# Norm scaling moved behind the products, reordered splits, a three-pass input product and spread late queries in a one-core transformer kernel

## The chip, the cores and the metric

The kernel is one program on one core of a Trainium2 chip. The metric is the device time of one execution in microseconds (us), median of three runs. Everything is fp32 with a sequence of 256 tokens and a model width of 1024.

## The reference, cut to what matters

Two layers of a first kind are followed by one layer of a second kind.

```python
def rms_norm(x, g):
    y = x * lax.rsqrt(jnp.mean(x * x, axis=-1, keepdims=True) + 1e-6)
    return y * g

for layer in range(2):
    x = x + 0.5 * swiglu(rms_norm(x, norm_ffn1[layer]), gate, up, down)   # swiglu: (silu(x@gate) * (x@up)) @ down
    xn = rms_norm(x, norm_mix[layer])
    x = x + mix(xn @ w_in) @ w_out[layer]       # layer 0: stick-breaking and block attention, layer 1: forgetting and dilated
    x = x + 0.5 * swiglu(rms_norm(x, norm_ffn2[layer]), gate, up, down)
# last layer
u = rmsnorm(x, g_mix) @ w_in                    # 2336 columns for two branches, 2048 for their gates
x = x + (gated rwkv7 recurrence and latent attention of u) @ w_out
h = rmsnorm(x, g_ffn)
q = h @ w_q                                     # 8 heads, top 16 of 128 x 128 keys each
x = x + sum_e gate_e * gelu(expert_u[e] . h) * expert_v[e]    # rows gathered for each token
x = x + sigmoid(rmsnorm(x) @ w_ple_gate) * (p @ w_ple_proj)   # side projection, then a final norm
```

## The kernel before

**Layout.** `xT` holds x transposed, eight chunks of 128 channels by 256 tokens. Weights stream from HBM through a ring of six slots of 1 MB (`ring`, filled by SP at L628, each fill waiting until the slot's last reader is done: `freed`). Every matmul is issued at L704.

**Split products.** The four feed-forward stages (`ffn(0)` to `ffn(3)`) and the two input products of the mixers (`layer`) split both operands into a high and a low fp32r part and take three passes (`mm3`: high by high, low by high, high by low). ACT makes the high part of a weight slot (L1384 in an FFN, L1391 in a mixer), DVE the low part (L1756, L1761). The gate and up weights have two pairs of buffers, the down weights one pair; ACT waits for `pair_used` before it overwrites a pair.

**Norms 0 to 5** stand ahead of the four FFNs and the two mixers. In order: DVE adds the last product to `xT` in four pieces (L1809 or L1816); ACT squares each piece (L1405); PE sums the squares over channels with a matmul by ones (`ssq`); ACT takes the inverse root by Ln and Exp (L1409, L1411, `rstd`); DVE multiplies x by the gain and by `rstd` (L1775); ACT takes the high part (L1415, `xh`), DVE the low part (L1779, `xl`); PE starts the next product.

**An FFN** has 22 chunks of 128 hidden channels in 11 groups of two. PE takes gate and up of chunk c, then down of chunk c - 1. ACT takes the silu of the gate bank (L1432), DVE the product with the up bank (L1792), ACT its high part (L1434), DVE its low part (L1795). After each even chunk both engines split one down slot, after each odd one a gate and an up slot. The order on each engine is the order written.

**A mixer's input product** has 12 slots. ACT evicts the query and key banks (L1520), DVE the value banks (L1913).

**The last layer's input product** (`second_in`) takes plain fp32 matmuls on `xn`, straight from the ring: nine slots of 256 columns and one of 32. ACT evicts (L1570) and DVE forms shifted sums after 5, 10 and 15 of the 19 pieces.

**The experts** run over 16 units of (128 tokens, one head). POOL gathers 16 u rows of a unit and, between them, 16 v rows of the unit before (L2356), 512 KB each, into 7 and 8 buffers. DVE takes the dot products with the u rows (L2234), ACT the softmax weights and gelu (table loads at L1693 and L1697), DVE the weights of the unit before after its fourth u row (L2221). ACT makes diagonal matrices (L1705) and PE adds diagonal times v row (`weighted_rows`). Queries and scores of six heads come first. Those of heads 6 and 7 and the side projection come in one block behind `weighted_rows(0)`, on PE and on ACT.

## Time and profile before

| | |
|---|---|
| median of three runs | 2450.94 us (2449.79 to 2454.59) |
| profiled execution | 2459.51 us, its span 2457.8 us |
| granted TensorE clock, mean | 0.925 |
| PE busy | 2106.7 us, 86% of the span |
| DVE, ACT, POOL busy | 1200.8, 787.8, 678.1 us |
| chain that ended last | PE 68%, POOL 10%, issue 6%, DVE 6%, DMA 4%, ACT 3% |

The chain says which engine the end waited for at each moment. A share of busy time says less, since the stages have different limits. The sum of a change is best made stage by stage, from the windows and the timeline at the places where PE or POOL stands still.

### The profile page before, as it was taken

What the parts mean: (1) busy time and instruction counts of PE and PEld (TensorE: products, weight loads), DVE (VectorE), ACT (ScalarE), POOL (GpSimd) and SP (SyncE); (2) the same over time, 40 slices, a digit from 0 to 9 for tenths busy, and PEclk for the clock granted to TensorE, in tenths of its full rate; (3) what the DMA queues carried; (4) which work ended last, traced back from release to release, by engine and by line L of the source; (5) the groups of instructions that cost most, each with busy time, mean ns of one, the idle gap of its engine ahead of it and who ended that gap; (6) DMA issues with size and microseconds to landing.
All of it is one profiled execution on the core that took longest, in us unless ns stands there. A gap on an engine that the chain in (4) does not pass through costs nothing.

```text
span 2457.8 us, 34543 instructions
## 1 busy us (share of the span) xinstructions
PE 2106.7 (86%) x13812; PEld 1680.0 (68%) x13812; DVE 1200.8 (49%) x2250; ACT 787.8 (32%) x1321; POOL 678.1 (28%) x702
## 2 busy tenths in 40 slices
PE   7999989999999999999995999986867667667677
PEld 7999878998999878999773887872422222223235
DVE  5455426445455434453336443285465566566432
ACT  4444535335344533443133223121222121212122
POOL 0000010000001000000006321047477777777770
PEclk9999999999999959999996997998888989878999
DMA  8554316554554305553420100579599999999990
GB/s 293 190 191 129 119 52 206 188 171 155 188 183 142 121 1 169 184 191 116 124 76 17 36 20 19 173 258 396 201 374 342 360 373 366 346 373 364 358 371 31
DMA packets 253787, 489.56 MB, mean 199 GB/s; under 512 B 13872, under 2 KB 173136, under 8 KB 253536
## 3 DMA queue, kind: packets, MB, share of 16 engines
q0 software_dynamic: 73888, 268.53, 29.2%
q1 hardware_dynamic: 176016, 214.32, 26.9%
q10 hardware_dynamic: 3760, 5.02, 0.6%
q8 instruction: 84, 1.38, 0.2%
q14 instruction: 39, 0.32, 0.0%
HBM read 486.74 MB, written 1.05 MB: 198 GB/s over the span
## 4 chain that ended last, share of the span: by engine, by line
PE 68%; POOL 10%; issue 6%; DVE 6%; DMA 4%; ACT 3%; another core or an unknown queue 1%; DVEq 0%; ACTq 0%; POOLq 0%
PE bank L704 67%; POOL arena_sb L2356 8%; POOL con_sb L2356 2%; DMA con_sb<-peer_v,arena_sb 1%; DMA arena_sb<-peer_u,arena_sb 1%; DVE parts_sb L1756 1%; DMA arena_sb<-peer_v,arena_sb 1%; DVE sq_sb L1775 1%; PE bank L851 1%; DVE xl_sb L1779 1%; ACT parts_sb L1384 1%; DVE arena_sb L2023 0%; DVE arena_sb L2103 0%; DMA xT_sb<-xT 0%
## 5 line engine op out<-in xcount | busy, mean ns | idle before, releaser
L704 PE MATMUL bank<-arena_sb 64*64 64x64 f32 (+8 forms) x3704 | 554.9, 338 | 195.2 <-ACT arena_sb L1705 119.3
L704 PE MATMUL bank<-xh_sb,parts_sb 128*128 128x256 f32 x3328 | 608.4, 285 | 19.0 <-DVE xl_sb L1779 11.9
L704 PEld LDWEIGHTS bank<-arena_sb 64*64 64x64 f32 (+4 forms) x3704 | 330.8, 172 | 415.6 <-issue 259.9
L704 PEld LDWEIGHTS bank<-xh_sb,parts_sb 128*128 128x128 f32 x3328 | 515.2, 190 | 29.6 <-issue 19.1
L704 PE MATMUL bank<-xl_sb,parts_sb 128*128 128x256 f32 x1664 | 469.5, 282 | 0.0
L2234 DVE CUSTOM_DVE_ANT_0 sq_sb<-arena_sb 128x1024 f32<-128x1024 f32 x256 | 309.6, 1224 | 265.2 <-DMA arena_sb<-peer_u,arena_sb 249.1
L1756 DVE TENSOR_TENSOR parts_sb<-ring_sb,parts_sb 128x2048 fp32r<-128x2048 f32 x132 | 298.6, 2290 | 192.2 <-ACT parts_sb L1384 192.2
L2356 POOL DMA_INDIRECT arena_sb<-peer_u,arena_sb x256 | 272.1, 1063 | 194.7 <-DVE arena_sb L2204 110.6
L704 PEld LDWEIGHTS bank<-xl_sb,parts_sb 128*128 128x128 f32 x1664 | 316.5, 190 | 0.0
L1384 ACT ACTIVATE parts_sb<-ring_sb 128x2048 fp32r<-128x2048 f32 x132 | 247.9, 1910 | 96.5 <-PE bank L704 95.1
L704 PE MATMUL bank<-xn_sb,ring_sb 128*128 128x256 f32 (+1 forms) x1200 | 271.1, 386 | 8.4 <-DVE xn_sb L1775 4.9
L704 PEld LDWEIGHTS bank<-xn_sb,ring_sb 128*128 128x128 f32 (+1 forms) x1200 | 229.3, 193 | 47.0 <-issue 14.4
L704 PE MATMUL bank<-h_high_sb,parts_sb 128*128 128x256 f32 x1408 | 256.2, 283 | 1.6 <-DVE parts_sb L1756 1.6
L704 PE MATMUL bank<-con_sb,arena_sb 128*128 128x512 f32 (+1 forms) x512 | 185.3, 511 | 52.2 <-DMA con_sb<-peer_v,arena_sb 50.2
L704 PEld LDWEIGHTS bank<-h_high_sb,parts_sb 128*128 128x128 f32 x1408 | 218.2, 190 | 2.3 <-DVE parts_sb L1756 2.2
L1705 ACT ACTIVATE arena_sb<-con_sb,arena_sb 128x128 f32<-128x128 f32 x256 | 90.2, 395 | 387.9 <-PE bank L704 158.6
L2356 POOL DMA_INDIRECT arena_sb<-peer_v,arena_sb x160 | 181.9, 1137 | 84.3 <-PE bank L704 43.0
L704 PE MATMUL bank<-h_low_sb,parts_sb 128*128 128x256 f32 x704 | 198.6, 282 | 0.0
L704 PEld LDWEIGHTS bank<-con_sb,arena_sb 128*128 128x128 f32 (+1 forms) x512 | 73.6, 176 | 159.6 <-issue 159.6
L1432 ACT ACTIVATE sgate_sb<-bank 128x256 f32<-128x256 f32 x88 | 33.8, 384 | 324.4 <-PE bank L704 324.4
L704 PEld LDWEIGHTS bank<-h_low_sb,parts_sb 128*128 128x128 f32 x704 | 134.1, 191 | 0.0
L2356 POOL DMA_INDIRECT con_sb<-peer_v,arena_sb x96 | 117.7, 1226 | 37.7 <-issue 24.1
(246 smaller groups left out, 1718.6 us busy)
## 6 DMA issues: line engine op xcount, KB each, us to landing
ring_sb<-ffn_w_gate SPq DMA_DIRECT2D x44, 1024.0 KB, 5.5
ring_sb<-ffn_w_up SPq DMA_DIRECT2D x44, 1024.0 KB, 6.6
ring_sb<-ffn_w_down SPq DMA_DIRECT2D x44, 1024.0 KB, 4.9
ring_sb<-w_in SPq DMA_DIRECT2D x17, 1024.0 KB, 5.3
ring_sb<-w_in_ab SPq DMA_DIRECT2D x12, 1024.0 KB, 5.2
ring_sb<-w_out SPq DMA_DIRECT2D x12, 1024.0 KB, 5.1
ring_sb<-w_in_cd SPq DMA_DIRECT2D x12, 1024.0 KB, 5.4
ring_sb<-peer_w_q SPq DMA_DIRECT2D x8, 1024.0 KB, 5.4
```

The source lines that it names most:

```text
L704: return pe.matmul(dst, lhsT, rhs, start=start, stop=stop_, skip_group_check=loose)
L851: ins = pe.transpose(b[:, dst : dst + P], pr[:, src : src + P], ident)
L1384: act.activation(whi(kind, g), ring[:, k % RING, :], ACT.Copy).then_inc(hi_ready, 1)
L1432: act.activation(sgate[:, c % 2, :], bank[4 + c % 2][:, 0:T], ACT.Silu).then_inc(silu_ready, 1)
L1705: act.activation(DG[n % ND], ident, ACT.Copy, scale=WT[:, tb, 16 * h + e : 16 * h + e + 1]).then_inc(S("diag_ready"), 1)
L1756: dve.tensor_tensor(wlo(kind, g), ring[:, k % RING, :], whi(kind, g), ALU.subtract).then_inc(split_ready, 1)
L1775: dve.scalar_tensor_tensor(out=raw[:, k, :], in0=xT[:, k, :], scalar=V(name, c0 + k), in1=rstd[:, :], op0=ALU.mult, op1=ALU.mult).then_inc ...
L1779: dve.tensor_tensor(xl[:, k - 2, :], sq[:, k - 2, :], xh[:, k - 2, :], ALU.subtract).then_inc(xn_ready, 1)
L2234: dve.tensor_tensor_reduce(JUNK[n % 2], UROW[n % NU], HTOK[:, tb, :], 1.0, 0.0, ALU.mult, ALU.add, DOTS[:, tb, 16 * h + e : 16 * h + e + 1 ...
L2356: pool.indirect_dma_start(out=row[n % len(row)], out_offset=None, in_=A[table][0], in_offset=bass.IndirectOffsetOnAxis(ap=EIDX[:, tb, 16 * ...
```

## The change

**Norms 0 to 5.** The product no longer waits for the inverse root. ACT writes `xh` as the high part of x times gain, straight from `xT` and ahead of the squares; DVE makes `xl` in one operation (x times gain minus `xh`), between the residual pieces. PE takes the first gate product (or the first value half) and only then the sum of squares. The root is applied where the product leaves its bank. In an FFN, DVE scales gate and up together (128x512) and the silu and the product read the result in SBUF. In a mixer, DVE evicts queries and keys times `rstd`, and values times a column of it that PE makes by two small matmuls (`rcol`). The squares and `MIX` get places of their own in the arena.

**Splits.** The first slot of a mixer and the first gate and up slots of `ffn(2)` are split after chunk 20 of the FFN before; those of `ffn(1)` and `ffn(3)` by DVE ahead of the residual; the second up slot after chunk 0.

**Last layer's input product.** Nine slots are split (two pairs of buffers) and take three fp32r passes; `xn` is split by ACT and DVE after the norm.

**Experts.** Query pieces 12 to 15 stand behind `weighted_rows(0)` to `(3)`, one each, and the two halves of the side projection behind `(4)` and `(5)`.

```diff
-        MIX = xn
+        MIX = view(24064, KC, T)
+        SQX = {n: view(0 if n in (1, 4) else 22016, KC, T) for n in range(6)}
+        RCOL = small[:, 160:162]
+        GU = [sgate, hT]
...
+        LATE = {0: ("query", 12), 1: ("query", 13), 2: ("query", 14), 3: ("query", 15), 4: ("ple", 0), 5: ("ple", 4)}
...
+                            if c == 0 and j + kk == 0:
+                                release(first)
...
+                        if c == 0 and j == 0:
+                            norm(n)
...
+                        if s == 0 and half == 0:
+                            norm(1 + 3 * l)
+                        if s == 0 and half == 1:
+                            b = fill_begin(pe, ("rcol", l))
+                            pe.wait_ge(S("rstd_ready"), 2 + 3 * l)
+                            for tb in range(2):
+                                ins = mm(b[:, tb : tb + 1], rstd[0:1, tb * P : (tb + 1) * P], C("ones", 1)[0:1, :], True, True)
+                            fill_end(ins, ("rcol", l))
...
+                                first, ins = mm3(b[:, 0:T], w[0][:, kk, cols], w[1][:, kk, cols], x2h[:, kk, :], xl[:, kk, :],
+                                                 kk == 0, kk == KC - 1)
...
+                    if u in LATE:
+                        kind, m = LATE[u]
+                        if kind == "query":
+                            query(m)
+                        else:
+                            projection(m)
...
+            def high_in2(s):
+                k, base = at["in2",] + s, SPLIT0["in2",]
+                act.wait_ge(slot_loaded[k % RING], 16 * (k // RING + 1))
+                if s > 1:
+                    act.wait_ge(pair_used, base + s - 1)
+                act.activation(in2_hi(s), ring[:, k % RING, :], ACT.Copy).then_inc(hi_ready, 1)
...
-                    high_qkv(n // 3, 0)
-                if f is not None and f > 0:
-                    if n in (2, 5):
-                        take(act, ("y", n // 3, 0))
+                if n in (2, 5):
+                    take(act, ("y", n // 3, 0))
                     high(f, "gate", 0)
                     high(f, "up", 0)
                 act.preload_act_table_set("natural_log_exp_and_others")
+                if n <= 5:
+                    name, c0 = norm_g[n]
+                    for m in range(4):
+                        residual_done(act, n, [m])
+                        for k in (2 * m, 2 * m + 1):
+                            act.activation(xh[:, k, :], xT[:, k, :], ACT.Copy, scale=V(name, c0 + k)).then_inc(xh_ready, 1)
+                    if n == 0:
+                        high(0, "gate", 0)
                 for m in range(4):
                     residual_done(act, n, [m])
-                    act.activation(sq[:, 2 * m : 2 * m + 2, :], xT[:, 2 * m : 2 * m + 2, :], ACT.Square).then_inc(sq_ready, 1)
-                if n == 0:
-                    high(0, "gate", 0)
+                    dst = SQX[n] if n <= 5 else sq
+                    act.activation(dst[:, 2 * m : 2 * m + 2, :], xT[:, 2 * m : 2 * m + 2, :], ACT.Square).then_inc(sq_ready, 1)
+                if n > 5:
+                    root(n)
...
-                high(f, "up", 1)
+                root(n)
...
+                    act.wait_ge(scaled, base + c + 1 + 4 * i)
+                    act.activation(gate, gate, ACT.Silu).then_inc(silu_ready, 1)
                     act.wait_ge(hraw_ready, base + c + 1 + 4 * i)
-                    act.activation(HH[:, c % 2, :], hT[:, c % 2, :], ACT.Copy).then_inc(hh_ready, 1)
+                    act.activation(HH[:, c % 2, :], h, ACT.Copy).then_inc(hh_ready, 1)
+                    if c == 0:
+                        high(f, "up", 1)
                     for kind, g in splits_after(c):
                         high(f, kind, g, i)
+                    if c == CHUNKS - 2 and f in (0, 2):
+                        high_qkv(f // 2, 0)
+                    if c == CHUNKS - 2 and f == 1:
+                        high(2, "gate", 0)
+                        high(2, "up", 0)
...
-                    if s >= 4:
-                        for _, _, m in chunks_of(l, s):
-                            b = take(act, ("qk", l, m))
-                            give(act.activation(QK[:, m, :], b[:, 0:T], ACT.Copy), ("qk", l, m))
...
+                for k in range(KC):
+                    act.wait_ge(xn_ready, KC * 6 + k + 1)
+                    act.activation(x2h[:, k, :], xn[:, k, :], ACT.Copy).then_inc(S("x2h_ready"), 1)
+                high_in2(1)
...
+            def low_x(n, m):
+
+                name, c0 = norm_g[n]
+                for k in (2 * m, 2 * m + 1):
+                    dve.wait_ge(xh_ready, KC * n + k + 1)
+                    dve.scalar_tensor_tensor(out=xl[:, k, :], in0=xT[:, k, :], scalar=V(name, c0 + k), in1=xh[:, k, :],
+                                             op0=ALU.mult, op1=ALU.subtract).then_inc(xn_ready, 1)
...
-                    dve.wait_ge(silu_ready, base + c + 1 + 4 * i)
+                    gate, h = GU[c % 2][:, 0, :], GU[c % 2][:, 1, :]
+                    dve.wait_ge(gu_ready, base + c + 1 + 4 * i)
                     if base + c >= 2:
                         dve.wait_ge(h_ready, base + c - 1 + 4 * i)
-                    dve.tensor_tensor(hT[:, c % 2, :], sgate[:, c % 2, :], bank[4 + c % 2][:, T : 2 * T],
-                                      ALU.mult).then_inc(hraw_ready, 1)
+                    dve.tensor_tensor(GU[c % 2][:, :, :], bank[4 + c % 2][:, :].rearrange("p (a b) -> p a b", a=2),
+                                      rstd[:, :].unsqueeze(1).broadcast_to([P, 2, T]), ALU.mult).then_inc(scaled, 1)
+                    dve.wait_ge(silu_ready, base + c + 1 + 4 * i)
+                    dve.tensor_tensor(h, gate, h, ALU.mult).then_inc(hraw_ready, 1)
                     dve.wait_ge(hh_ready, base + c + 1 + 4 * i)
-                    dve.tensor_tensor(HL[:, c % 2, :], hT[:, c % 2, :], HH[:, c % 2, :], ALU.subtract).then_inc(h_ready, 1)
+                    dve.tensor_tensor(HL[:, c % 2, :], h, HH[:, c % 2, :], ALU.subtract).then_inc(h_ready, 1)
+                    if c == 0:
+                        low(f, "up", 1)
...
+                    if m and n < 5:
+                        low_x(n + 1, m - 1)
+                if n < 5:
+                    low_x(n + 1, 3)
...
+                            give(dve.tensor_scalar(VT[:, j % 2, 4 * (j // 2) : 4 * (j // 2) + 4, 0:HD],
+                                                   b[:, 0:T].rearrange("p (a c) -> p a c", a=4), RCOL[:, j % 2 : j % 2 + 1],
+                                                   None, ALU.mult), ("v", l, j))
...
+                    else:
+                        for _, _, m in chunks_of(l, s):
+                            b = take(dve, ("qk", l, m))
+                            give(dve.tensor_tensor(QK[:, m, :], b[:, 0:T], rstd[:, :], ALU.mult), ("qk", l, m))
+                    if s == 0:
+                        low_qkv(l, 2)
...
+                low(2 * l + 1, "gate", 0)
+                low(2 * l + 1, "up", 0)
+                residual(("y", l), 3 * l + 2)
...
+                for k in range(KC):
+                    dve.wait_ge(S("x2h_ready"), k + 1)
+                    dve.tensor_tensor(xl[:, k, :], xn[:, k, :], x2h[:, k, :], ALU.subtract).then_inc(S("x2_ready"), 1)
+                low_in2(1)
...
+                    for s in ((2, 3), (4, 5, 6), (7, 8))[g]:
+                        low_in2(s)
```

## Rows read from the trace of the kernel before

**Rows 1.** The page's slices: DMA share in 40 equal parts of the span.

```profile
DMA  8554316554554305553420100579599999999990
```

**Rows 2.** Windows: us, PE, PEld, DVE, ACT, POOL busy, PE clock, DMA share, GB/s.

```profile
212.50:228.15 15.65, 11.68 (x67) 10.29 (x65) 11.32 (x21) 10.55 (x16) 0.00 (x0) 0.89 0.20 67
368.50:390.60 22.10, 17.94 (x113) 15.81 (x111) 18.55 (x25) 12.72 (x18) 0.00 (x0) 0.92 0.71 224
567.40:591.00 23.60, 17.51 (x114) 16.11 (x112) 18.66 (x26) 14.93 (x22) 0.00 (x0) 0.93 0.49 160
591.00:767.80 176.80, 176.75 (x1488) 176.76 (x1489) 83.00 (x73) 72.47 (x73) 0.00 (x0) 1.00 0.54 175
1720.00:1750.00 30.00, 24.23 (x88) 18.18 (x89) 6.56 (x25) 11.76 (x30) 1.45 (x2) 0.79 0.16 56
1748.00:2400.00 652.00, 453.57 (x951) 183.76 (x951) 370.73 (x909) 127.72 (x304) 498.40 (x447) 0.88 0.97 360
```

**Rows 3.** Windows of PE alone around norm 1 and norm 6: PE busy, clock, DMA.

```profile
216.10:219.50 3.40, 0.62 (x4) 1.00 0.81 265
219.50:223.50 4.00, 3.89 (x17) 0.59 0.11 37
1154.40:1156.00 1.60, 0.03 (x1) 1.00 0.00 0
```

**Rows 4.** Timeline of norm 1: start, us, engine, line, operation, idle before.

```profile
210.51 2.85 DVE L1809 SCALAR_TENSOR_TENSOR xT_sb<-bank,xT_sb 128x512 f32<-128x512 f32 x4 [1.83 <-PE bank L704]
...
212.47 3.61 PE L704 MATMUL bank<-sq_sb,con_sb 128*128 128x256 f32 x16
...
216.12 0.47 ACT L1409 ACTIVATE std_sb<-bank,con_sb 128x256 f32<-128x256 f32 x1 [2.10 <-PE bank L704]
...
218.84 0.36 PE L704 MATMUL bank<-parts_sb,xh_sb 128*128 128x256 f32 x1 [2.75 <-DVE xl_sb L1779]
...
228.15 0.39 PE L704 MATMUL bank<-parts_sb,xh_sb 128*128 128x256 f32 x1 [1.06 <-DVE parts_sb L1761]
```

**Rows 5.** Timeline of an odd and an even chunk inside ffn(1).

```profile
462.42 4.49 DVE L1756 TENSOR_TENSOR parts_sb<-ring_sb,parts_sb 128x2048 fp32r<-128x2048 f32 x2 [1.39 <-ACT parts_sb L1384]
...
467.83 0.39 ACT L1432 ACTIVATE sgate_sb<-bank 128x256 f32<-128x256 f32 x1 [3.64 <-PE bank L704]
...
470.70 1.92 ACT L1384 ACTIVATE parts_sb<-ring_sb 128x2048 fp32r<-128x2048 f32 x1 [1.57 <-PE bank L704]
```

**Rows 6.** Timeline of the first splits of ffn(1) up to its first down product.

```profile
386.31 1.91 ACT L1384 ACTIVATE parts_sb<-ring_sb 128x2048 fp32r<-128x2048 f32 x1
...
388.26 2.29 DVE L1756 TENSOR_TENSOR parts_sb<-ring_sb,parts_sb 128x2048 fp32r<-128x2048 f32 x1 [1.39 <-ACT parts_sb L1384]
...
390.60 0.51 PE L704 MATMUL bank<-h_high_sb,parts_sb 128*128 128x256 f32 x2 [0.55 <-DVE parts_sb L1756]
```

**Rows 7.** Groups by line and form: count, busy us, mean ns, idle before.

```profile
L1405 ACT ACTIVATE sq_sb<-xT_sb 128x512 f32<-128x512 f32 x40 | 23.9, 626 | 68.9 <-DVE xT_sb L1816 66.5 <-DVE xT_sb L1809 1.7
...
L1697 ACT ACT_TABLE_LOAD x16 | 20.5, 1283 | 0.3
...
L1415 ACT ACTIVATE xh_sb<-sq_sb 128x256 fp32r<-128x256 f32 x48 | 19.8, 417 | 13.6 <-DVE sq_sb L1775 13.6
...
L1903 DVE TENSOR_TENSOR arena_sb<-bank,con_sb 128x512 f32<-128x512 f32 x8 | 5.5, 686 | 4.0 <-PE bank L704 3.9
```

**Rows 8.** Timeline of norm 6 and the last layer's input product.

```profile
1155.42 3.25 DVE L1775 SCALAR_TENSOR_TENSOR xn_sb<-xT_sb,vec_sb,rstd_sb 128x256 f32<-128x256 f32 x8 [3.71 <-ACT rstd_sb L1411]
...
1156.05 65.97 PE L704 MATMUL bank<-xn_sb,ring_sb 128*128 128x256 f32 x304 [1.62 <-DVE xn_sb L1775]
```

**Rows 9.** Timeline of the experts: the late block, and a later unit's start.

```profile
1719.91 0.66 ACT L1679 ACTIVATE arena_sb<-bank 128x256 f32<-128x256 f32 x2 [34.29 <-remote]
...
1748.25 0.94 POOL L2356 DMA_INDIRECT arena_sb<-peer_v,arena_sb  x1 [30.87 <-PE bank L704]
...
1881.64 10.97 PE L704 MATMUL bank<-arena_sb 128*128 128x512 f32 x20 [11.30 <-ACT arena_sb L1705]
```

**Rows 10.** Waits from 1760 to 2400 us: total, times, longest.

```profile
ACT arena_sb L1705 <- issue: 86.9, 43, 12.4
```

More of the change, by code:

```diff
@@ L1411, in norm, with ffn @@
                 act.activation(rstd[:, :], std[:, :], ACT.Exp, scale=-0.5).then_inc(S("rstd_ready"), 1)
[L1412 to L1417 removed]
+            def ffn(f, n):
                 base = CHUNKS * f
@@ L1534, in layer @@
                 if l == 1:
-                    b = take(act, ("forget", 1))
+                    emptied(act, ("forget", 1))
                     act.wait_ge(S("bf_loaded"), 16)
-                    chain.link(act, act.activation(FG[0:8, 0, :], b[0:8, 0:T], ACT.Abs, bias=small[0:8, 40:41]))
+                    chain.link(act, act.activation(FG[0:8, 0, :], FG[0:8, 2, :], ACT.Abs, bias=small[0:8, 40:41]))
                     chain.link(act, act.activation(FG[0:8, 0, :], FG[0:8, 0, :], ACT.Exp, scale=-1.0))
@@ L1705, in experts @@
                         act.activation(DG[n % ND], ident, ACT.Copy, scale=WT[:, tb, 16 * h + e : 16 * h + e + 1]).then_inc(S("diag_ready"), 1)
[L1706 to L1711 removed]
+                    if u in LATE:
+                        kind, first = LATE[u]
+                        if kind == "query":
+                            query_out(first)
+                        else:
+                            for m in range(first, first + 4):
+                                b = take(act, ("pp", m))
+                                give(act.activation(PLE[:, m, :], b[:, 0:T], ACT.Copy), ("pp", m))
                     if h == 7:
@@ new lines, in low_x, with ffn @@
+            def low_x(n, m):
[4 more added lines that the diff above has]
+                                             op0=ALU.mult, op1=ALU.subtract).then_inc(xn_ready, 1)
+            def ffn(f, n):
+                base = CHUNKS * f
+                if f == 0:
+                    for m in range(4):
+                        low_x(0, m)
+                    low(0, "gate", 0)
+                    low(0, "up", 0)
@@ L1799, in ffn @@
+                    if c == CHUNKS - 2 and f == 1:
+                        low(2, "gate", 0)
+                        low(2, "up", 0)
                 for c in range(3):
```

222 lines of the change are left out of this document (110 added, 112 removed).

## The prediction

> **What bounds the kernel now.** The windows come first. Inside an FFN PE is busy for 176.75 of 176.80 us and pulls 1488 matmuls, 0.119 us each; DVE works 83 us there and ACT 72 [rows 2]. So PE sets the FFNs, and only where PE stands still or works less can time be won. It stands still at the norms: 15.65 us pass around norm 1, 22.10 around norm 2 and 23.60 around norm 3, with 11.68, 17.94 and 17.51 of PE in them, part of it at the low clock [rows 2]; norm 4 repeats norm 1 and norm 5 norm 2 to 0.1 us, so these are five places. The slices show the other bound: the DMA engines are 9 tenths busy from slice 27 on, but for one slice with 5 [rows 1]. The experts are bound by gathering (share 0.97 over 652 us), and between 1720 and 1750 the share is 0.16 [rows 2]. That hole is 0.84 x 30 = 25.2 us of lost transfer. POOL waits 30.87 us there for a v buffer, and ACT 34.29 us before it evicts the first late query [rows 9].
>
> **Norm 1, the pattern.** Before, the last down product ends at 212.47, the sum of squares takes 3.6, the root starts at 216.12, the first product at 218.84, and slot 1 of the mixer starts at 228.15 after a wait for its split [rows 4]. After, DVE has from 210.51 on four residual pieces (2.85 together [rows 4]) and eight low parts. Each is one operation of the kind of L1775, eight of which take 3.25 [rows 8]. ACT's eight high parts at 0.42 [rows 7] run between them. The last low part is there at 210.51 + 2.85 + 3.25 = 216.6, the first half product ends at 217.0, fed at DVE's pace. The squares (4 x 0.63 [rows 7]) are ready by then but for the last, and PE sums them until 220.6. The second half takes 24 x 0.119 = 2.85, the column of the root 0.3: slot 1 could start at 223.7.
>
> The split moved into chunk 20 costs something. In an even chunk the down slot's high part starts 2.9 us after the silu and takes 1.92 [rows 5]. DVE then has its low part and one more, 4.49 together [rows 5], so it is free 9.3 us after the silu of chunk 20, and chunk 21's bank is full after 72 x 0.119 = 8.6. Chunk 21's chain is now scaling (priced by L1903, 0.69 [rows 7]), silu 0.39, and three operations of 0.42: some 2.5 us. PE wants it 2.85 after the bank is full; it comes 0.5 late. Slot 1 starts at 224.2 instead of 228.15: 3.9 won, twice (norms 1 and 4).
>
> **Norms 2 and 5.** From the end of the output product E (368.5) only one residual piece and four low parts are left on DVE, about 2.6 us. First gate product ends E + 3.0, sum of squares E + 6.6, up product E + 9.5. Then the splits bind. Chunk 0's chain up to its high part takes 2.0; ACT makes two high parts (1.91 each [rows 6]) and DVE two low parts behind the first (4.49): E + 9.5 + 2.0 + 1.9 + 4.5 = E + 17.9, that is 386.4. PE could start the down product at E + 15.2, so a wait of 2.7 takes the place of the 0.55 before. Before it started at 390.60 [rows 6]: 4.2 won, twice.
>
> **Norm 3.** Two slots are split in chunk 20, so DVE has 6.7 us of low parts and the last down product comes 2.7 late. From E = 570.1 the pattern of norm 1 gives the up product's end at E + 11.0 and the splits as above E + 19.4 = 589.5, against 591.0 [rows 2]: 1.5 won. Norm 0 waits for the first weights; I take nothing, at most 2. Sum of the five: 17.7 us.
>
> **The steady FFN is not slowed.** Scaling adds 0.73 per chunk to DVE. After an odd chunk the two low parts end at 466.91 and the next silu starts at 467.83 [rows 5]: 0.9 free. In an even chunk ACT waits 1.57 us for the down buffer [rows 5], so 1.1 more of chain is free. What hides the 88 scalings (61 us of DVE) is this idle time; without that cover each group would pay up to 1.5 us, 66 in all.
>
> **The clock.** In norm 1 PE stood still for 2.75 us [rows 4], and the granted clock then fell to a mean of 0.59 for 4 us, mostly the lower level, 1.2 GHz [rows 3]. A gap of 1.6 us ahead of norm 6's product left it at 1.00 [rows 3]. Before, the low clock cost little, since DVE's pace ruled then. After, the gaps in the first product are each below 1 us, but it is followed by PE-bound work. A fall costs half of 3.5 us. I take 1.7 us at norms 1 and 4 and nothing elsewhere: 3 (bounds 0 and five falls, 8.5). The Trainium skill's "TensorE: Matmul & The Clock Gate" (section on the HAM clock gate) says that the low rate is the default and sustained activity releases it; by that rule alone a half-fed first product would lose the clock each time, and the norms would give 9 us instead of 15.
>
> **Norms together: 17.7 - 3 = 14.7 won.**
>
> **Last layer's input product.** 152 plain matmuls took 65.97, 0.434 each [rows 8]. 144 of them become three passes of 0.119: 144 x (0.434 - 0.356) = 11.2 won. The start is later: DVE has a low part of a slot first (2.29), which ends 1.1 after the old start of `xn`, then all eight pieces of `xn` (3.25) before the first low part (0.42); in place of 0.6 after 1155.42 PE starts 4.9 after it: 4.3 lost. PE then stood still for 5.9 us, so the low clock costs 1.7. In the stage a slot takes PE 5.7 us and ACT plus DVE 4.7. The shifted sums (about 5 us on DVE, ahead of the low parts of slots 4 and 7) make those two 0.6 late each. 11.2 - 4.3 - 1.7 - 1.2 = 4.0 won (1 to 6.5). The waits on `split_ready` instead of PE free ring slots earlier; SP's loads stay ahead.
>
> **Evictions.** DVE takes the query and key banks. Per slot it then has 0.8 + 2.3 + 0.75 + 2.1 = 6 us against 7.4 of PE with the two small products. The forget gate adds one link, 0.4 lost.
>
> **Experts.** Late pieces now have the gap that PE has at a unit's start, 11.30 us of waiting for ACT's diagonals [rows 9]. Behind a query (8 x 0.434 = 3.5 us, 7 at the low clock) ACT needs an eviction, two table loads (1.28 each [rows 7]) and two short ones, 3.6. So 7.7 is free and a piece fits, barely with scores behind it. The first one meets ACT's late start. If ACT again goes on only at 1719.91 [rows 9], its diagonals come at 1724 and POOL goes on at 1726 instead of 1748.25. POOL's wait shrinks from 30.9 to 8.5, and the transfers in flight ran until about 1725 (0.16 x 30 = 4.8 after 1720), so 2.5 us of hole stays. The other five pieces I give 1.7 together. 25.2 - 4.2 = 21 won. Bounds: 25 if all is hidden, 8 if each of the five costs another 3.
>
> **The sum.** 14.7 + 4.0 - 0.4 + 21 = 39.3. The profiled execution took 2459.51, span 2457.8, which is 0.35% above the median; the sum is a difference of stages and I put it on the median: 2450.9 - 39.3 = 2411.6.
>
> **Rivals.**
> - *The late pieces cost again.* ACT waits of up to 12.4 us for nothing that the trace shows stand between its diagonals (86.9 in 43 waits [rows 10]). If such a wait meets most pieces, the hole returns in parts and only 4 of 21 us are won: 2429. For it: the 34.29 [rows 9]. Against: POOL has 8 v rows of room.
> - *Everything fits.* No fall of the clock, no wait of ACT at the first piece, sums in second_in hidden: 17.7 + 7 + 25 = 50: 2401; with norm 0, 2398.
> - *Slower.* The place is ACT behind `weighted_rows(0)` to `(5)`: a piece sits ahead of the next unit's gelu, which now waits for PE. Its price is piece 7 + wait 12.4 + 3.6 - 11.3 = 11.7 per unit, 70 in six, against 25.2 + 18.3 won: 2451 + 27 = 2478. It decides from 7.3 us per piece. Against: the gap of 11.3.
> - *The chain of a chunk binds.* If five operations with their hand-overs take 1 us more than priced, over 44 groups up to 0.6 each: 26 lost, 2438. Against: rows 5.
> - *The clock falls at each norm* (the skill's rule, above): 6 more lost, 2418; it lies within the forecast's range.
> - *No effect*: the transitions only move their wait and pieces cost as much as the block: 2451.
>
> **Chances.** Forecast (2403 to 2422) 0.50, the clock's case 0.08 in addition, late pieces 0.15, all fits 0.12, the chain 0.05, slower 0.06, no effect 0.04. To leave out no more than 2 in 10 the range goes from 2394 to 2432. What a measurement of this kernel can tell from no change is about 0.2%, 5 us: faster 0.90, same 0.04, slower 0.06.
>
> **What the profile after would show.** Windows from the down product's end to slot 1 of the mixer of 11.7 us instead of 15.7, and 18 instead of 22.1 at norms 2 and 5. At the first down product of `ffn(1)` a PE wait of about 2.7 us for DVE; in chunk 21 of `ffn(1)` one of 2.7. No wait of PE inside the FFNs. The input product in 54 to 57 us, starting about 5 later. No DMA hole above 5 us around the former 1720 to 1750, and POOL waits on PE below 10 us. The prediction is wrong if POOL's waits come back at the first six units, if PE waits inside every FFN group, or if the clock stays low through `ffn`'s first chunk.

## The result and the profile after

The changed kernel takes 2426.85 us, median of four runs (2423.39 to 2431.57), against 2452.77 for the kernel before in the same session. The ratio is 0.9893, with a 95% interval of 0.9866 to 0.9921: 26 us faster, where 39 were forecast. The time lies inside the range (2394 to 2432) but above the likeliest case's own (2403 to 2422).

The profiled execution took 2426.50, span 2424.8, 33.0 less than the span before. The page's slices of the changed kernel, in the order PE clock and DMA share:

```profile
PEclk9999999999999969999987998998998898789899
DMA  8554416554554404554320100579998999999990
```

The slice of 5 tenths inside the experts [rows 1] is gone. What happened elsewhere is read from milestones. This table is put together from the starts and ends of timeline rows (first and last down product of each FFN on PE, last residual piece on DVE, the first 64-row product of an attention, the last layer's first sum of squares, the first sum of squares behind the recurrence); "stage" is the difference of neighbours, in us.

```
stage                                  before    after     won
start to first down product of ffn(0)   35.68    39.09    -3.41
rest of ffn(0)                         176.95   179.68    -2.73
norm 1 and the input product            85.69    81.25     4.44
attention 0, output product             70.35    70.05     0.30
norm 2 to the first down product        21.93    17.79     4.14
rest of ffn(1)                         176.95   182.77    -5.82
norm 3 to the first down product        23.49    18.99     4.50
rest of ffn(2)                         176.96   179.18    -2.22
norm 4 and the input product            95.86    91.54     4.32
attention 1, output product             88.24    83.29     4.95
norm 5 to the first down product        21.93    17.79     4.14
rest of ffn(3)                         176.94   178.43    -1.49
norm 6 and the last input product       73.76    69.98     3.78
latent attention                        96.45    96.10     0.35
recurrence and branches                271.90   267.61     4.29
experts                                814.22   799.30    14.92
side projection, final norm             50.49    51.96    -1.47
```

Attention 1, the recurrence and the ending, 8 of the 33 us, are not put down to the change. Nothing in the recurrence or the ending was edited, and from the end of `ffn(3)` to the last residual ahead of the experts nine traces with the same program there last from 433.7 to 446.9 us. Attention 1 lasts 88.2, 88.0 and 82.7 us in three traces of kernels with the old norms and 82.9 to 83.8 in the eleven with the new ones. It goes with the clock there: its mean is 0.69, 0.69 and 0.75 in the first three and 0.73 in the changed kernel. So 25 us of the trace can belong to the change, near the 26 between the medians.

**Norms 1 and 2.** Windows of the changed kernel around norm 1 and norm 2, from the last product before to slot 1 of the mixer and to the first down product (us, then PE, PEld, DVE, ACT, POOL busy, PE clock, DMA share, GB/s):

```profile
218.61:229.81 11.20, 10.48 (x70) 9.52 (x68) 6.10 (x10) 10.18 (x15) 0.00 (x0) 1.00 0.01 1
369.90:387.86 17.96, 15.09 (x114) 14.47 (x112) 10.67 (x12) 11.43 (x14) 0.00 (x0) 1.00 0.76 246
```

They were 15.65 and 22.10 [rows 2]; 11.7 and 18 were forecast. The clock is 1.00 in the whole of norm 1: PE's gaps in the first product are 0.34 and 0.37 us, where one of 2.75 stood ahead of it [rows 4]. PE's waits for the splits, in the timeline of the changed kernel:

```profile
39.09 0.79 PE L715 MATMUL bank<-h_high_sb,parts_sb 128*128 128x256 f32 x2 [6.14 <-DVE parts_sb L1815]
...
215.63 0.50 PE L715 MATMUL bank<-h_high_sb,parts_sb 128*128 128x256 f32 x2 [0.48 <-DVE h_low_sb L1864]
...
387.86 0.50 PE L715 MATMUL bank<-h_high_sb,parts_sb 128*128 128x256 f32 x2 [2.87 <-DVE parts_sb L1815]
...
566.09 0.80 PE L715 MATMUL bank<-h_high_sb,parts_sb 128*128 128x256 f32 x2 [2.68 <-DVE h_low_sb L1864]
```

The waits of 2.87 (2.7 forecast), 2.68 (2.7) and 0.48 (0.5) were foreseen, the 6.14 in `ffn(0)` was not. And each of the long ones has a second price. In windows of PE alone (us, PE busy, clock, DMA share, GB/s) it is seen behind three of them, and not yet in the one before the first of these:

```profile
384.00:387.80 3.80, 0.99 (x9) 1.00 0.24 56
387.80:391.50 3.70, 3.64 (x19) 0.58 1.07 392
589.60:593.60 4.00, 3.98 (x20) 0.57 1.06 393
39.00:43.00 4.00, 3.91 (x18) 0.50 1.08 368
```

The granted clock is at or near the lower level, 1.2 GHz, for 3 to 4 us once PE works again. `ffn(3)` has no other disturbance and takes 178.43 instead of 176.94: 1.5 us each time.

**Norm 0.** ACT's timeline in the changed kernel, from the root to the second silu:

```profile
24.98 0.42 ACT L1460 ACTIVATE rstd_sb<-std_sb 128x256 f32<-128x256 f32 x1
24.99 0.33 ACTq L1470 DMA_DIRECT2D con_sb<-con  x1
25.36 0.45 ACTq L1471 DMA_DIRECT2D arena_sb<-w_in_cd  x1
25.84 4.21 ACTq L1472 DMA_DIRECT2D small_sb<-b_f  x1
30.08 1.28 ACT L1473 ACT_TABLE_LOAD   x1 [4.68 <-issue]
31.38 0.42 ACT L1478 ACTIVATE sgate_sb<-sgate_sb 128x256 f32<-128x256 f32 x1
```

Chunk 0 was scaled by 28.07, yet its silu starts at 31.38. Three transfer issues that the diff does not touch stand between the root and the table load, and the last alone takes 4.21. Before, the root came at 14.65 and the issues ran beside splits that had to be made anyway, well ahead of the first silu (ACT's timeline before):

```profile
21.80 2.68 ACTq L1427 DMA_DIRECT2D small_sb<-b_f  x1
23.07 3.70 ACT L1384 ACTIVATE parts_sb<-ring_sb 128x2048 fp32r<-128x2048 f32 x2
...
30.20 0.39 ACT L1432 ACTIVATE sgate_sb<-bank 128x256 f32<-128x256 f32 x1 [2.13 <-PE bank L704]
```

Now the root comes late and they are in the chain.

**Experts.** POOL's longest waits on PE in the changed kernel, in order of time (timeline of POOL):

```profile
1796.49 1.75 POOL L2457 DMA_INDIRECT arena_sb<-peer_v,arena_sb  x1 [3.37 <-PE bank L715]
...
1846.04 0.94 POOL L2457 DMA_INDIRECT arena_sb<-peer_v,arena_sb  x1 [8.12 <-PE bank L715]
```

The wait of 30.87 [rows 9] is gone, and the one at the place of the first piece did not come. The 8.12 stands behind the fourth unit. There ACT evicts the second late score bank 8.8 us after the query, in place of 1.3 at the first:

```profile
1734.67 0.38 ACT L1739 ACTIVATE arena_sb<-bank 128x256 f32<-128x256 f32 x1 [1.31 <-PE bank L715]
...
1837.25 0.38 ACT L1739 ACTIVATE arena_sb<-bank 128x256 f32<-128x256 f32 x1 [8.82 <-remote]
```

PE had ended those scores at 1830.4. Nothing in the trace shows what ACT waited for until 1837.25.

### The profile page after: what moved, and what is told of

It reads as the page before. It is cut to its first block, busy times and chain, and to the rows that moved or that the text cites. A ratio compares the mean times of both kernels' runs of the same rounds, so it can differ in the third digit from the quotient of the medians.

```text
span 2424.8 us, 34935 instructions
## 1 busy us (share of the span) xinstructions
PE 2086.9 (86%) x13964; PEld 1668.9 (69%) x13964; DVE 1281.7 (53%) x2342; ACT 795.9 (33%) x1306; POOL 678.9 (28%) x702
## 4 chain that ended last, share of the span: by engine, by line
PE 68%; POOL 10%; DVE 7%; issue 6%; DMA 4%; ACT 3%; another core or an unknown queue 1%; ACTq 0%; DVEq 0%; POOLq 0%
PE bank L715 67%; POOL arena_sb L2457 8%; POOL con_sb L2457 2%; DMA con_sb<-peer_v,arena_sb 2%; DVE parts_sb L1815 1%; DMA arena_sb<-peer_u,arena_sb 1%; DMA arena_sb<-peer_v,arena_sb 1%; ACT parts_sb L1416 1%; PE bank L866 1%; DVE arena_sb L2127 0%; DVE xn_sb L1828 0%; DVE parts_sb L1834 0%; DVE xT_sb L1885 0%; DVE xl_sb L1841 0%
## 5 line engine op out<-in xcount | busy, mean ns | idle before, releaser
L715 PE MATMUL bank<-arena_sb 64*64 64x64 f32 (+8 forms) x3704 | 544.3, 333 | 180.6 <-ACT arena_sb L1762 81.8
L715 PE MATMUL bank<-xh_sb,parts_sb 128*128 128x256 f32 x3328 | 603.5, 284 | 17.0 <-DVE parts_sb L1815 16.4
L715 PEld LDWEIGHTS bank<-arena_sb 64*64 64x64 f32 (+4 forms) x3704 | 320.7, 168 | 398.2 <-issue 285.6
L715 PE MATMUL bank<-xl_sb,parts_sb 128*128 128x256 f32 x1808 | 508.9, 281 | 0.0
L715 PEld LDWEIGHTS bank<-xl_sb,parts_sb 128*128 128x128 f32 x1808 | 342.5, 189 | 0.0
L715 PE MATMUL bank<-h_high_sb,parts_sb 128*128 128x256 f32 x1408 | 264.2, 288 | 18.4 <-DVE parts_sb L1815 14.7
L715 PEld LDWEIGHTS bank<-h_high_sb,parts_sb 128*128 128x128 f32 x1408 | 224.6, 196 | 19.8 <-DVE parts_sb L1815 15.6
L715 PE MATMUL bank<-xn_sb,ring_sb 128*128 128x256 f32 (+1 forms) x656 | 148.6, 385 | 3.4 <-DVE xn_sb L1828 3.2
L715 PEld LDWEIGHTS bank<-xn_sb,ring_sb 128*128 128x128 f32 (+1 forms) x656 | 123.4, 190 | 26.9 <-issue 9.0
L715 PE MATMUL bank<-arena_sb,ring_sb 128*128 128x256 f32 (+2 forms) x592 | 134.1, 390 | 2.6 <-issue 2.6
L715 PEld LDWEIGHTS bank<-arena_sb,ring_sb 128*128 128x128 f32 (+2 forms) x592 | 114.1, 193 | 23.2 <-issue 5.0
```

The source lines that it names most:

```text
L715: return pe.matmul(dst, lhsT, rhs, start=start, stop=stop_, skip_group_check=loose)
```

## The experiments

They ran on three chips, here B, C and D, on which the kernel before takes 2432, 2448 and 2437 us. The first session's is called A; it is not known whether it is one of them (C is nearest to it). So times are compared by ratio, or within one chip. Each chip stands for one session, so that chip and hour cannot be told apart. Medians in us, ratios to the kernel before on the same chip as on record (a quotient of two medians can differ from them by 0.001):

```
kernel                  chip   median  before    ratio  95% interval
e1_late_block            B    2419.83  2432.14   0.9943  0.9922 to 0.9963
e2_plain_input           B    2409.14  2432.14   0.9907  0.9884 to 0.9931
e3_down_first            B    2393.89  2432.14   0.9846  0.9820 to 0.9872
e4_issues_first          B    2401.55  2432.14   0.9877  0.9852 to 0.9903
c1_after                 C    2425.62  2447.68   0.9901  0.9873 to 0.9929
e5_all_orders            C    2399.36  2447.68   0.9803  0.9777 to 0.9829
e6_chunk19               C    2412.13  2447.68   0.9862  0.9835 to 0.9889
e7_before_late           C    2426.49  2447.68   0.9911  0.9886 to 0.9936
c2_after                 D    2404.72  2437.06   0.9869  0.9838 to 0.9901
e8_block_again           D    2417.60  2437.06   0.9921  0.9891 to 0.9951
e9_before_late_again     D    2414.82  2437.06   0.9904  0.9868 to 0.9941
e10_norms_only           D    2422.10  2437.06   0.9930  0.9899 to 0.9960
```

### The late pieces together again: e1

```diff
-        LATE = {0: ("query", 12), 1: ("query", 13), 2: ("query", 14), 3: ("query", 15), 4: ("ple", 0), 5: ("ple", 4)}
+        LATE = {0: [("query", 12), ("query", 13), ("query", 14), ("query", 15), ("ple", 0), ("ple", 4)]}
-                    if u in LATE:
-                        kind, m = LATE[u]
+                    for kind, m in LATE.get(u, []):
```

> The changed kernel with the four late query pieces and the side projection back in one block behind the first unit; all else as changed. If spreading them won what the prediction says (21 us), this takes 2427 + 21 = 2448 us and DMA has its hole of some 25 us back. Read from the two traces (the stretch from the last layer's merged product to the final residual shrank by 14.9 us) it is 2427 + 15 = 2442 us. Rival, the pieces cost as much spread as together: within 3 us of 2427.

The ratio is 0.9943, about half a per cent above the changed kernel's on the other chips (0.9869 to 0.9901); the changed kernel itself was not run on B. So it speaks against "as much spread as together", and c2 and e8, the same two kernels on one chip, rule that out (below). The size was not settled by it. Its trace has a hole back (a DMA share of 0.80 from 1690 to 1750), but POOL's longest wait there is 16.4 us, not 30.9.

### The input product in plain fp32: e2

```diff
-                        pe.wait_ge(split_ready, SPLIT0["in2",] + s + 1)
-                        w = [part.rearrange("p (k n) -> p k n", k=KC) for part in (in2_hi(s), in2_lo(s))]
+                    k = at["in2",] + s
+                    have(k)
+                    width = 32 if s == 9 else 256
+                    w = slot(k, KC, width)
...
-                                first, ins = mm3(b[:, 0:T], w[0][:, kk, cols], w[1][:, kk, cols], x2h[:, kk, :], xl[:, kk, :],
-                                                 kk == 0, kk == KC - 1)
+                                ins = mm(b[:, 0:T], w[:, kk, half * P : (half + 1) * P], xn[:, kk, :], kk == 0, kk == KC - 1)
```

> The changed kernel with the last layer's input product in plain fp32 again, straight from the ring; all else as changed. The prediction's sum for this part is 4.0 us won (11.2 by the passes, less a later start, a fall of the clock and shifted sums): 2431 us, with PE's first product of that stage starting some 4 us earlier after the end of ffn(3) and the stage itself ending 4 us later. Rival, the three passes win their whole 11 us: 2438. Rival, splits and the later start eat it all: 2427 or below.

Too small for the ratio (0.9907), but the trace settles it. From the end of `ffn(3)` to the last layer's first sum of squares it takes 1215.85 - 1142.09 = 73.76 us, the 73.76 of before to the hundredth, as in the three other traces with plain products (e7, e9, e10); the changed kernel takes 69.98, and 69.96 to 70.48 in the other traces with three passes. The term is 3.8 us. The start and the two waits behind the shifted sums stand in the timeline of the changed kernel, where both were put, and a window of PE behind the start has the low clock:

```profile
1149.02 0.77 PE L715 MATMUL bank<-parts_sb 128*128 128x256 f32 x2 [5.71 <-DVE xl_sb L2053]
...
1174.20 0.50 PE L715 MATMUL bank<-parts_sb 128*128 128x256 f32 x2 [0.54 <-DVE parts_sb L1834]
...
1191.97 0.50 PE L715 MATMUL bank<-parts_sb 128*128 128x256 f32 x2 [0.54 <-DVE parts_sb L1834]
```

```profile
1149.02:1153.02 4.00, 4.00 (x19) 0.50 0.85 283
```

By these rows the start is 4.1 us later after the end of `ffn(3)` than before (9.17 for 5.08), the clock costs 2.0 and the two waits 1.1; 4.3, 1.7 and 1.2 were forecast.

### The first down slot ahead of the second up slot: e3

```diff
+            if (kind, g) in (("down", 0), ("up", 1)):
+                return 3 if kind == "down" else 4
...
+                    for kind, g in splits_after(c):
+                        high(f, kind, g, i)
                     if c == 0:
                         high(f, "up", 1)
-                    for kind, g in splits_after(c):
-                        high(f, kind, g, i)
```

DVE's order and SP's loads are swapped alike.

> The changed kernel with one order swapped on SP, ACT and DVE: after chunk 0 of each FFN the first down slot is split before the second up slot. In the trace PE waits 2.87 us for that split at norms 2, 3 and 5, and then runs for 3.7 us at a granted clock of 0.58. If the wait makes the clock fall, the wait shrinks to about 0.7, the clock stays at 1.00 and each of the three places gains 2.2 + 1.6 us; with norm 0 about 13 us in all: 2414 us. If the clock falls there whatever the wait is: 7 us, 2420. If the up slot is late in its place: no gain.

Ratio 0.9846: by its interval clearly under e1 (0.9943), and 0.3% under e4. Up to the experts e1 is the changed kernel on the same chip; `ffn(3)` ends at 1125.85 in e3's trace and at 1139.86 in e1's, 14.0 us apart where 13 were expected. In its timeline the wait at norm 2 is 0.66 us, and windows of PE before, behind and at the same place of `ffn(2)` keep the full clock:

```profile
382.65 0.50 PE L718 MATMUL bank<-h_high_sb,parts_sb 128*128 128x256 f32 x2 [0.66 <-DVE parts_sb L1818]
```

```profile
379.00:382.60 3.60, 2.99 (x26) 1.00 0.39 123
382.60:386.60 4.00, 3.94 (x33) 1.00 0.62 204
...
580.70:584.00 3.30, 3.28 (x27) 1.00 0.61 178
```

`ffn(3)` behind it takes 1125.85 - 948.92 = 176.93 again. Each of the three places gained 2.2 + 1.5, by the wait and by the clock: with the long wait the fall went too. At norm 0 the wait is still 3.79, with a fall behind it, since the issues are still there.

### ACT's issues ahead of the root: e4

```diff
-                root(n)
                 if f == 0:

                     act.dma_start(con[:, NFIRST:NCON], A["con"][:, NFIRST:NCON]).then_inc(S("masks_loaded"), 16)
...
+                root(n)
                 act.preload_act_table(ACT.Silu)
```

> The changed kernel with ACT's three transfer issues of the first FFN put ahead of the inverse root instead of behind it. In the trace ACT's first silu starts at 31.38 us, 3.3 after its input is scaled, behind issues that end at 30.05. If they are what delays it, it starts at about 28.1, PE's first down product at 35.8 instead of 39.1, and the time is 3.3 us less: 2424. If the order of the splits behind chunk 0 is the whole cause of norm 0's loss, the wait of 6.1 us stays and the time is 2427.

ACT's silu starts at 28.85 and the first down product at 36.57 (28.1 and 35.8 expected). In its timeline the slow issue now overlaps ACT's wait for the sum of squares:

```profile
18.73 3.35 ACTq L1471 DMA_DIRECT2D small_sb<-b_f  x1
25.23 0.47 ACT L1458 ACTIVATE std_sb<-bank,con_sb 128x256 f32<-128x256 f32 x1 [5.45 <-PE bank L715]
```

`ffn(0)` ends at 214.24 instead of 218.77: 4.5 won. The issues are worth 2.5 of it, the earlier down product, and not 3.3, since the root itself starts 0.8 later here (25.23 for 24.47). The other 2.0 are the clock, which does not fall behind the wait that is left, although that is 2.87 us long again (below, under hardware).

### The early splits behind chunk 19: e6, and all three orders: e5

Chunk 19 has no splits of its own: the last gate and up slots are split behind chunk 17. e6 moves the next stage's early splits there and swaps them with the last down slot in the ring's order.

```diff
-                return 3 * g + 4 if g < GROUPS - 1 else FFN_SLOTS - 1
-            return (max(3 * g - 1, 0)) + (kind == "up")
+                return 3 * g + 4 if g < GROUPS - 1 else FFN_SLOTS - 1 + (1, 2, 1, 0)[f]
+            return (max(3 * g - 1, 0)) + (kind == "up") - (f == 2 and g == 0)
...
-                    if c == CHUNKS - 2 and f == 1:
+                    if c == CHUNKS - 3 and f == 1:
                         high(2, "gate", 0)
                         high(2, "up", 0)
```

> The changed kernel with only the early splits moved from behind chunk 20 to behind chunk 19. If the wait of 2.68 us in ffn(1) and the low clock of 0.67 to 0.79 behind it come from the two extra splits, both go, and the two waits of 0.48 at the ends of ffn(0) and ffn(2) with them: 5 us less. If that wait comes from the chain of chunk 21 itself, nothing changes.

In its trace `ffn(1)` takes 566.86 - 388.42 = 178.44 from the first down product, instead of 182.77: the wait of 2.68 and the low clock behind it are gone, 4.3 us, and with the two of 0.48 (each of which had cost 0.7) 5.8. So the two extra splits made that wait. `ffn(3)` ends only 3.4 us earlier than in c1_after's trace, mostly since attention 0 lasts 71.3 us in it and 70.1 in the other; it varies so without e6's edit too (71.2 in c2_after). The median is 2412.13 against 2425.62 for the changed kernel beside it. That is more than 5.8; the experts, which e6 does not touch, last 787.0 in its trace and 802.2 in c1_after's (below).

e5 has the edits of e3, e4 and e6 together.

> Three orders changed together in the changed kernel: the first down slot ahead of the second up slot behind chunk 0, ACT's three issues ahead of the root, and the early splits of the next stage behind chunk 19, which has no splits of its own, instead of chunk 20 (with their places in the ring swapped). From the traces: 11 us at norms 2, 3 and 5, 7 at norm 0, 0.5 each at norms 1 and 4, and 2.7 + 1.6 at the end of ffn(1): 23 us less than the changed kernel, a ratio to before of 0.980. Rival, chunk 19's chain or the loads swapped in the ring are late instead: a new PE wait at down(19) or down(20), and no more than 16 us.

The ratio is 0.9803 where 0.980 was expected, 48 us under the kernel before and 26 under the changed one on the same chip. `ffn(3)` ends at 1116.51, in c1_after's trace at 1139.35: 22.8 us, 23 expected. Windows of the first three FFNs of e5, from the first down product on:

```profile
34.34:211.20 176.86, 176.86 (x1489) 176.85 (x1490) 102.05 (x97) 73.64 (x76) 0.00 (x0) 1.00 0.59 194
377.81:554.77 176.96, 176.96 (x1489) 176.95 (x1490) 104.33 (x99) 75.52 (x77) 0.00 (x0) 1.00 0.58 190
571.72:748.60 176.88, 176.88 (x1489) 176.87 (x1490) 102.06 (x97) 73.64 (x76) 0.00 (x0) 1.00 0.56 184
```

PE has no gap in them, with the scalings on DVE (102 us instead of 83 [rows 2]). The steady FFN is not slowed. e5 is the version that beats both kernels.

### The late pieces on the kernel before, and two by two: c1, e7, c2, e8, e9, e10

c1 and c2 are the changed kernel as it is. e7 and e9 are the kernel before with only the queries and the side projection spread:

```diff
-                    if u == 0:
-                        for h in range(FIRST_HEADS, 8):
-                            queries(h)
-                        projection()
+                    if u in LATE:
+                        kind, m = LATE[u]
+                        if kind == "query":
+                            query(m)
+                        else:
+                            projection(m)
```

> The changed kernel as it is, on the same chip as the three beside it, for a control. The four runs before this one stood on a chip where the kernel before takes 2432 us instead of 2451, and their expert stages were 770 to 773 us long with spread pieces and 794 with the block, against 799 and 814 in the first two traces. If the change is worth 21 us in the experts and the shortfall in the first trace of after was of that execution, the stage is near 770 here too and the ratio to before is 0.988 to 0.990; if the spread pieces cost again in every execution, POOL's wait of 8.1 us behind the fourth unit is back.

> The kernel before with only the late pieces spread over six units. The prediction's 21 us for the experts would give a ratio to before of 0.9915; the first pair of traces 15 us, 0.994. Rival, the pieces cost again where they are put: above 0.997.

c1's ratio is 0.9901, but its experts last 802.2 us, not some 770, and POOL's wait behind the fourth unit is back, at 11.7 us, with one of 10.7 behind a later unit. e7's ratio of 0.9911 is 21.8 us, almost the forecast's 21. But e1 (all but the spreading) had 14 us, and 36 is not what the whole change wins. So the four corners were run on one chip, e8 as e1, e10 with the edits of e1 and e2.

> The changed kernel again, beside the three kernels that make two by two of the change's halves on one chip (late pieces together or spread, the rest as before or as changed). With the prediction's terms the ratio would be 0.984; by the three comparisons so far 0.989 to 0.990.

> The changed kernel with the late block, on the same chip as the others. Theory that the halves add up: its gain and that of the kernel before with spread pieces (21.8 us measured) sum to the gain of the whole change; it then stands at 0.998 (some 4 us). The run before gave 0.9943 for it, which with 21.8 makes 36 us where the whole change gives 25. Rival: the two halves are worth less together, since POOL's waits that the spread pieces leave differ from chip to chip: 0.994 again.

> The kernel before with spread late pieces, again. Additive: 0.991 to 0.992. If its 21.8 us belonged to that chip or that hour: 0.994 or above.

> The changed kernel with the late block and the plain input product: what is left of the change is norms 0 to 5 and the splits. Prediction's terms: 14.7 won, less 0.4, a ratio of 0.994. Read from the traces stage by stage (norm 0 loses 6.1, norms 1 and 4 win 4.4 each, 2 and 5 win 4.1 each and lose 1.5 to the clock behind, norm 3 and the end of ffn(1) lose 1.3 together): 6 us, 0.9975.

c2 came at 0.9869 (expected 0.989 to 0.990 by the comparisons, 0.984 by the prediction's terms), e8 at 0.9921 (0.998 or 0.994), e9 at 0.9904 (0.991 to 0.992), e10 at 0.9930 (0.994 or 0.9975).

The kernel before spreads over 28 us in its 13 runs there, the four others over 7 to 21, so their medians tell more beside each other than by ratio. Spreading: 2417.60 - 2404.72 = 12.9 us. Three passes: 2422.10 - 2417.60 = 4.5. Norms: 2437.06 - 2422.10 = 15.0, with an interval of 10 to 25 by the ratio. The stage reading had expected 6, outside that interval. The traces bear the 6 out all the same: on D `ffn(3)` ends at 1146.53 in e9 (old norms) and at 1138.92 in e10 (new ones), 7.6 apart, of which 1.3 lie in attention 0. Against the two old kernels traced on A and C (1150.97 and 1149.87) it is 7.8 to 12.1 with attention 1's clock. No trace finds 15, and the kernel before has none on D; so the size of this part is open between 6 and 15.

The halves do not add up by the medians either: the spreading is 22.2 us by e9 against the kernel before and 12.9 by c2 against e8. The interval of e9's ratio alone is 9 us to either side, so this difference is not resolved; in the traces the experts last the same in both (772.4 in e9, 773.6 in c2).

The length of the experts, from the last residual piece ahead of them to the residual behind them, is the part that differs:

```
chip    block                          spread
A       814.2 (before)                 799.3 (after)
B       794.1 (e1)                     772.7 (e2)  769.9 (e3)  770.5 (e4)
C                                      802.2 (c1)  785.1 (e7)  787.0 (e6)  789.4 (e5)
D       785.3 (e8)  785.1 (e10)        773.6 (c2)  772.4 (e9)
```

On D the difference is 12, on A 15, on B 23 (with one trace of the block there, of e1); C has no trace with the block, and its four with spread pieces lie 17 apart. Waits of ACT and POOL in the experts tell the chips apart. In c1_after on chip C (total, times, longest):

```profile
ACT arena_sb L1762 <- PE bank L715: 126.8, 65, 6.6
ACT arena_sb L1762 <- issue: 93.5, 50, 11.4
...
POOL arena_sb L2457 <- PE bank L715: 30.8, 18, 11.7
...
ACT arena_sb L1739 <- remote: 8.7, 1, 8.7
```

In c2_after on chip D, the same program:

```profile
ACT arena_sb L1762 <- PE bank L715: 175.0, 123, 2.5
...
POOL arena_sb L2457 <- PE bank L715: 8.8, 29, 0.3
POOL con_sb L2457 <- PE bank L715: 4.9, 16, 0.3
```

On B and D ACT has no wait between its diagonals for which the trace shows nothing, on A (86.9 us [rows 10]) and C it has. Without them, POOL never waits more than 0.8 us on PE in the traces with spread pieces there. And the block itself costs less. The timelines of ACT and POOL in e8 at the block:

```profile
1687.90 0.38 ACT L1732 ACTIVATE arena_sb<-bank 128x256 f32<-128x256 f32 x1 [21.50 <-PE bank L715]
```

```profile
1716.71 0.94 POOL L2455 DMA_INDIRECT arena_sb<-peer_v,arena_sb  x1 [18.40 <-PE bank L715]
```

They are 34.29 and 30.87 in the trace of before [rows 9]. The window of e8 from 1690 to 1750 has a DMA share of 0.76, a hole of 14 us; c2's has 0.99.

## Why the prediction was right, and where its 13 us went

**Direction and mechanisms held; three sizes did not.** Of the 39.3 us forecast, the stages of the trace give 8.8 less in the norms and 6.1 less in the experts; the medians came out 13.4 short. That the trace shows as much as 33.0 is in part luck: 7.8 of them lie in stages that are not put down to the change. Point by point:

- *Norms 1 and 4*, 3.9 each by the steps, less 1.7 for a fall of the clock: measured 4.4, and 3.7 after the 0.7 that the split in chunk 20 costs. The chain on DVE and ACT came as worked out (window 11.20 for 11.7). The fall did not come; PE's gaps are 0.34 and 0.37 us there. The 0.4 for the forget gate cannot be read by itself: norm 4's stage, which holds it, wins 4.32 where norm 1's wins 4.44.
- *Norms 2 and 5*, 4.2 each: 4.14. The wait that takes the place of the old one is 2.87 for 2.7. The fall of the clock that the prediction put at norms 1 and 4 stands behind this wait, 1.5 each.
- *Norm 3*, 1.5 won: its waits came as sized (2.68 and 2.87 for 2.7), but with the two falls behind them 1.3 are lost (the end of `ffn(1)` to the start of the rest of `ffn(2)`: 5.82 lost, 4.50 won; the 1.5 that norm 2 had left is in the first, the one that norm 3 leaves follows).
- *Norm 0*, nothing lost, at most 2 won: 6.1 lost (3.4 by the later first down product, 2.0 by the clock, 0.7 by chunk 21). This is the step that failed. "Norm 0 waits for the first weights" was true of the products and not of ACT's queue. A step that was moved (the root) was moved past three issues, and what had run beside them now waits behind them. e4 shows the issues (2.5 of the 3.4, and the 2.0), e3 the order of the splits (2.3 of the 3.4, and 0.5 of the 2.0), e5 both with no loss left.
- *The norms together*: 14.7 forecast, 5.9 by the trace's stages (the sum of the rows from the start to `ffn(3)`, without the attentions), 15 by e10's medians, which no trace bears out. 3.4 of the shortfall are norm 0's later start and 5.1 the clock: 3 was taken for it (its own two falls of 1.7 make 3.4) and 8.1 is what the falls cost (2.0, four of 1.5 or 1.6), near the bound of 8.5 given for five. The rival "the clock falls at each norm" was right in number and wrong in place. The clock is 1.00 all through norm 1, whose first product is spread over 4.3 us where its 24 matmuls need 2.9. The Trainium skill's "TensorE: Matmul & The Clock Gate" (section on the HAM clock gate) says that the low rate is the default and that sustained activity releases it. That a product fed like this one loses the full rate was the prediction's own step from there, and norm 1 speaks against it.
- *Input product*: 4.0 forecast, 3.8 measured, by the parts named.
- *Steady FFN*: not slowed, as claimed; "the chain of a chunk binds" is out.
- *Experts*: 21 forecast; 15, 23 and 12 by the traces on A, B and D, 12.9 by the medians of D, 21.8 by e7 and 22.2 by e9, on the kernel before. The step that was mis-sized is the hole: all 25.2 us of it were put down to the block. ACT's wait of 34.29 ahead of it had no shown cause, and on chips without such waits it is 21.5 and the hole 14. The forecast used that wait once as a cost that stays (the first piece) and once as one that goes; it was of that execution or chip. In the changed kernel ACT evicts the first late query after 20.9 us, and the 2.5 us of hole kept for the first piece did not come.
- *The late pieces cost again* (2429, 0.15) is nearest in time and only in part the cause. On B and D POOL never waits more than 0.8 us on PE. On A and C waits of POOL of 8.1, 11.7 and 8.8 us stand behind the fourth unit in three traces (the changed kernel, c1, e5), each behind ACT's 8.7 to 8.8, and in two others of C with spread pieces (e6, e7) there is none. So a piece meets such a wait in some executions; why is not known.
- *Slower*, *no effect* and *everything fits* did not happen.

What stays open: why ACT stands still on some chips; what the norms are worth (6 by the traces, 15 by the medians of D); why the two halves measured against the kernel before (21.8 and 14, on D 22.2 and 19.5) add up to more than the whole; and whether attention 1's shorter spell at the low clock has to do with the new norms, which e9 makes doubtful (82.7 us with the old ones).

## What to carry to other kernels

When a step is moved later on an engine, list all that now stands between it and its user, issues included: three issues, the last of 4.2 us, that cost nothing beside splits cost 2.5 and a fall of the clock (2.0) in the chain. Price a PE gap like those of 2.7 to 2.9 us ahead of dense work here at its length plus 1.5, and put work that nobody waits for yet where an engine has none of its own (chunk 19) and behind what is awaited first (the down slot): three swaps of order, with no work removed, won as much as the change itself. A wait that has no cause in the trace is not a term: look at it in a second trace before it is counted as won.

## What the runs showed of the hardware that was not expected

- ACT's waits without a shown cause go by chip or session: between diagonals 75 to 97 us in 47 to 53 waits over the whole of each of the six traces of A and C, none in the eight of B and D. Three traces of A and C have a wait of 8.7 to 8.8 at the same score bank; it is 1.31 in seven other traces with spread pieces.
- The same gap does not always cost the clock. Behind waits of 2.86 or 2.87 at the first down product of `ffn(1)` to `ffn(3)` it fell in all 27 cases of nine traces (the rest of the FFN is 1.5 us longer each time). Behind the one of 2.87 in e4's `ffn(0)` it did not:

```profile
33.00:36.50 3.50, 0.69 (x6) 1.00 1.03 392
36.50:38.50 2.00, 1.93 (x16) 1.00 1.09 348
```

  Behind gaps of 0.66 and 0.67 it never did, in seven cases. In the kernels with the old norms, where a gap of 2.75 us stands ahead of the first product of norms 1 to 5, the clock fell at 12 of the 15 gaps of three traces; it stayed at 1.00 at norm 5 of the kernel before and at norms 1 and 2 of e9. The first is the window of the kernel before, the other two are e9's:

```profile
958.27:962.27 4.00, 3.50 (x18) 1.00 0.51 160
...
218.80:222.80 4.00, 3.49 (x18) 1.00 0.29 101
375.79:379.79 4.00, 3.52 (x18) 1.00 0.50 157
```

  A fall there cost nothing, as the prediction had it: the stage of norm 1 lasts 85.69 and 85.66 us with it (before, e7) and 85.66 without (e9).
- The chips differ by 0.8% in the kernel before (2432 to 2453), nearly as much as the change is worth; a stage that a trace times to 0.1 us on all of them (`ffn(3)`: 176.93 to 176.95 without a fall) says more than the total.
